# Eleven groups of unread TensorE products taken out ahead of waits, in a two-block float32 model on one core

## The reference, cut to what matters

```
for li in range(2):                                  # first block
    hl = rmsnorm(xl, norm1_g) * (1 + sc1) + sh1
    p  = hl @ w_in                                   # split into latent q, latent kv, rope key, q, k, v, conv
    q  = rmsnorm(p_q, q_norm_g) @ w_uq               # 6 heads of 96
    kv = rmsnorm(p_kv, kv_norm_g) @ w_ukv            # 6 heads, 64 + 64
    a, b, cv = mla(q, kv), swa(...), short_conv(...) # 6 + 6 heads, softmax over up to 512 keys
    xl = xl + g1 * (concat(a, b, cv) @ w_o)
    h  = rmsnorm(xl, norm2_g) * (1 + sc2) + sh2
    aff = softmax(h @ router_w)                      # 16 experts
    top_aff, idx = top_k(aff.T, 32)                  # every expert takes its 32 best tokens
    xl = xl + g2 * scatter(expert_ffn(h[idx]) * top_aff)
x = rmsnorm(xl, final_norm_g)
for layer in range(2):                               # second block
    h = rms_norm(x, norm1_g)
    y = [stick_breaking(h), rwkv7(h), moba(h), hgrn2(h)]
    x = x + (sum over n of sigmoid(h @ w_gate[n]) * (y[n] @ w_branch[n])) @ w_out
    h2 = rms_norm(x, norm2_g)
    x = x + (silu(h2 @ w_ffn_gate) * (h2 @ w_ffn_up)) @ w_ffn_down
return rms_norm(x, final_g)
```

## Time and profile before

| What | Value |
|---|---|
| median of 3 runs | 2405.73 us (2404.16 to 2406.09) |
| the profiled execution's own time | 2400.18 us |
| span of the profiled execution | 2398.1 us |
| TensorE busy | 2207.2 us, 92% of the span |
| VectorE busy | 732.0 us, 31% |
| ScalarE busy | 451.8 us, 19% |
| GpSimd busy | 99.4 us, 4% |
| granted TensorE clock, mean | 0.979 of full |
| moved by DMA | 434.99 MB, mean 181 GB/s |

### The profile page before, as it was taken

One profiled execution on the slowest core, in us unless ns is written; L12 is line 12 of the kernel. 1 busy time (PEld: TensorE's weight loads), 2 busy tenths in 40 slices (PEclk: granted clock), 3 DMA queues, 4 the chain that ended last, 5 costly groups with the idle time before them and its releaser, 6 DMA issues.

```text
span 2398.1 us, 26783 instructions
## 1 busy us (share of the span) xinstructions
PE 2207.2 (92%) x11455; PEld 1605.1 (67%) x11455; DVE 732.0 (31%) x1519; ACT 451.8 (19%) x970; POOL 99.4 (4%) x97
## 2 busy tenths in 40 slices
PE   5898999999889989988798989999999899999998
PEld 2334445665465466544677878888887788888887
DVE  2107723132233731112355423300014444141001
ACT  3003423111121430101134112100003321210000
POOL 1000000000010010000100200000000011000000
PEclk8999999999999999999999999999999999999999
DMA  8532422799922529998532214443543231344352
GB/s 326 208 121 90 151 105 106 311 425 425 415 87 76 176 118 377 427 426 360 186 106 100 100 47 141 141 140 125 157 157 139 72 106 43 120 152 142 124 152 76
DMA packets 172886, 434.99 MB, mean 181 GB/s; under 512 B 6202, under 2 KB 64482, under 8 KB 156130
## 3 DMA queue, kind: packets, MB, share of 16 engines
q1 hardware_dynamic: 171632, 430.90, 48.2%
q10 hardware_dynamic: 1138, 2.39, 0.3%
HBM read 432.23 MB, written 1.05 MB: 181 GB/s over the span
## 4 chain that ended last, share of the span: by engine, by line
PE 78%; DMA 10%; DVE 7%; ACT 3%; issue 1%; POOL 1%; ACTq 0%; DVEq 0%; POOLq 0%
PE bank L274 75%; DMA ring<-in_exp_w_up 4%; DMA ring<-in_exp_w_gate 2%; DMA cst<-in_exp_w_up 1%; PE bank L693 1%; PE bank L518 1%; DMA ring<-in_w_in 1%; POOL arena L578 1%; DVE rstd L602 1%; DMA cst<-in_exp_w_gate 1%; DMA arena<-in_x 1%; DVE arena L658 0%; DVE bank L673 0%; ACT h L597 0%; ACT arena L663 0%
## 5 line engine op out<-in xcount | busy, mean ns | idle before, releaser
L274 PE MATMUL bank<-h,ring 128*128 128x256 f32 (+1 forms) x4064 | 1003.0, 407 | 31.9 <-DMA ring<-in_w_in 11.0
L274 PEld LDWEIGHTS bank<-h,ring 128*128 128x128 f32 x4064 | 770.6, 191 | 249.7 <-issue 128.5
L274 PE MATMUL bank<-arena 128*64 128x256 f32 (+13 forms) x1840 | 325.7, 377 | 51.1 <-ACT arena L663 12.9
L274 PEld LDWEIGHTS bank<-arena 128*128 128x128 f32 (+4 forms) x1840 | 223.2, 193 | 139.3 <-issue 75.8
L274 PE MATMUL bank<-arena,ring 128*128 128x256 f32 x1216 | 264.1, 379 | 6.7 <-DVE arena L2161 3.9
L274 PEld LDWEIGHTS bank<-arena,ring 128*128 128x128 f32 x1216 | 230.3, 190 | 40.5 <-DVE arena L2161 4.7
L663 ACT ACTIVATE arena<-bank 128x256 f32<-128x256 f32 (+5 forms) x265 | 117.6, 461 | 631.1 <-PE bank L274 599.6
L274 PE MATMUL bank<-ring,arena 128*64 128x256 f32 x1344 | 154.3, 384 | 22.1 <-DMA ring<-in_exp_w_up 13.8
L658 DVE COPY arena<-bank 128x256 f32<-128x256 f32 (+7 forms) x116 | 62.3, 539 | 320.3 <-PE bank L274 267.0
L274 PEld LDWEIGHTS bank<-ring,arena 128*64 128x64 f32 x1344 | 97.5, 138 | 85.0 <-DMA ring<-in_exp_w_up 20.3
L578 POOL TENSOR_TENSOR arena<-arena 128x256 f32<-128x256 f32 (+1 forms) x60 | 53.7, 895 | 1805.2 <-ACT arena L571 1803.7
(11 more groups left out here) (278 smaller groups left out, 1466.9 us busy)
## 6 DMA issues: line engine op xcount, KB each, us to landing
ring<-in_w_in SPq DMA_DIRECT2D x32, 2048.0 KB, 7.9
ring<-in_ada_w SPq DMA_DIRECT2D x24, 2048.0 KB, 10.8
ring<-in_exp_w_up SPq DMA_DIRECT2D x22, 2048.0 KB, 15.8
ring<-in_exp_w_gate SPq DMA_DIRECT2D x20, 2048.0 KB, 15.2
ring<-in_exp_w_down SPq DMA_DIRECT2D x20, 2048.0 KB, 16.0
ring<-in_w_ffn_down SPq DMA_DIRECT2D x16, 1408.0 KB, 7.0
ring<-in_w_ffn_gate SPq DMA_DIRECT2D x10, 2048.0 KB, 7.7
ring<-in_w_ffn_up SPq DMA_DIRECT2D x10, 2048.0 KB, 7.7
```

The source lines that it names most:

```text
L274: return PE.matmul(o, lhsT, rhs, start=(k == 0), stop=(k == n - 1))
```

## The change

It deletes `keep_busy` and its eleven calls. Nothing is put in their place.

```
@@ -297,13 +297,6 @@
-        def keep_busy(pe, n):
-
-            b = take(pe, "idle", turn[0])
-            for _ in range(2 * n):
-                mm(b[:, 0:2 * P], ones, cst[:, 0:2 * P], 0, 1)
-            holder[(turn[0] - 1) % rotating[0]] = None
@@ -866,7 +859,6 @@
                 last.then_inc(*tensor.mark("mean", l, name))
-            keep_busy(pe, 4)
             pe.wait_ge(*vector.at("latent", l, "q"))
@@ -911,7 +902,6 @@
             mean_tensor(pe, TQ, ("n2", l))
-            keep_busy(pe, 5 if l < L - 1 else 3)
             join(tensor, pe, ("mixed", l))
@@ -1239,7 +1229,6 @@
                 htok_tensor(pe, l, i)
-            keep_busy(pe, 5)
             pe.wait_ge(*vector.at("pos", l))
@@ -2233,7 +2221,6 @@
                 mean_tensor(pe, S, after_ffn(l))
-                keep_busy(pe, 3)
```

More of the change, by code:

```diff
@@ L299, in take @@
             return banks[b]
[L301 to L306, removed]
         def bank(*key):
```

## The result

| | before | after |
|---|---|---|
| median | 2405.91 us (2404.16 to 2410.88, 4 runs) | 2423.59 us (2421.02 to 2427.55, 4 runs) |
| ratio | | 1.0069, interval 1.0050 to 1.0087 |
| profiled execution, its span | 2400.18, 2398.1 us | 2427.55, 2425.7 us |
| granted clock, mean | 0.979 | 0.961 |

What follows compares the result with a forecast made beforehand. TensorE, with 78% of the chain of waits, was taken to bound the kernel; removed products counted nothing, but half-clock resumes summed to 9.1 us, added to the 2405.73 median for 2414.8 us, range 2409 to 2419.5.

Steps and rivals of the forecast that it cites:

- B: Wait ahead of attention's first scores, layer 0 (225.43 us): newly half clock, late scores delay the attention chain; 1.7 us.
- C: Wait ahead of the router, layer 0 (391.10 us): resume price 1.9 less 0.86 us of ScalarE slack; 1.0 us.
- D: Wait ahead of the dense gather, layer 0 (408.20 us): 1.9 plus 0.1 for small transposes, not absorbed by DMA; 2.0 us.
- F: Wait ahead of the dense latent q products, layer 1 (765.61 us): resume newly at half clock; 1.9 us.
- H: Wait ahead of the router, layer 1 (886.09 us): newly half clock, less 0.33 us of slack; 1.6 us.
- E: Wait after the scatter, layer 0 (681.63 us): ScalarE delivers tiles so slowly that half clock keeps up; 0.
- G: Wait ahead of attention, layer 1 (786.89 us): already resumes at half clock, can only start it earlier; 0.3 us.
- A: Wait ahead of the latent q, layer 0 (197.54 us): already resumes at half clock, so has paid; 0.3 us.
- I: Wait ahead of the gather, layer 1 (899.10 us): already resumes at half clock, so has paid; 0.3 us.
- J: Wait after the scatter, layer 1 (1154.29 us): already 8.73 us idle and half clock before; 0.
- The clock holds through about 5 us: Rival, chance 0.12: only idle times above 6 us cost the clock, C and F, 2.9 us; 2408.6 us.
- Half clock lasts: Rival, chance 0.12: half clock persists through sparse attention and transposes, up to 3 us more in two or three places.

Runs made afterwards that it cites:

- more_all: Against the kernel before: longer unread groups at eight of the eleven waits, plus groups at seven more places; 2387.80 us, ratio 0.9923.
- turns_only: Against the kernel before: the eleven calls still take a bank and a turn but issue no product; 2419.95 us, ratio 1.0067.
- products_only: Against the kernel before: all 90 products stay but take no turn, so later tiles have the changed kernel's banks; 2407.23 us, ratio 1.0001.
- out_d: Against the kernel before: only the unread group at D taken out; 2407.84 us, ratio 1.0006.
- out_aegijk: Against the kernel before: the groups at A, E, G, I, J and at the very end taken out; 2413.25 us, ratio 1.0033.
- out_bcdfh: Against the kernel before: the groups at B, C, D, F and H taken out; 2416.66 us, ratio 1.0043.
- out_b: Against the kernel before: only the group at B taken out; 2408.75 us, ratio 1.0008.
- out_aj: Against the kernel before: only the groups at A and J taken out; 2409.30 us, ratio 1.0010.
- half: Against the kernel before: every unread group has half its products; 2418.24 us, ratio 1.0052.
- more_tails: Against more_all: groups added ahead of the first tokens' wait and the last three heads in the first block's three attentions; 2386.85 us, ratio 0.9921.

## Why the prediction was right or wrong

**Bound and cover: right.** The 90 products cost nothing where they stood. All idle times grew by the group's length with the same releaser, and more_all adds 204 records to the 11455 of before and is 17.5 us faster.

**The banks: right at 0.** turns_only has the whole loss and products_only none of it.

**The clock as the cause: right.** Behind the waits at B, C, D, F and H it is 0.50, or a mean with it, as said. The spans of the eleven traces of the table above reach from 2398.1 to 2425.7 us; less the cost of half clock, 37.8 to 66.9 us, all lie between 2355.1 and 2360.3.

**C, 1.0 forecast, wrong in size.** From 7.82 to 9.37 us for the router and 1.56 up to D. The slack of 0.86 us was taken off a price that was too low, see F.

**D, 2.0 forecast, right:** 1.96 us up to F, E's nothing included. The first 34 records of the gather take 9.85 us in out_d and 10.55 in after instead of 8.50, so 1.35 to 2.05. **E, 0: right**: D to F is 357.05 us in out_aegijk, without E's group, and 357.24 to 357.90 where both stand.

**F, 1.9 forecast, under:** 18.83 for 16.30 us, 2.5. **H, 1.6 forecast, under:** 6.12 for 3.95, 2.2. At both, and at C, the price of one resume was too low. I took it from G, where a mean clock of 0.76 over 7.1 us makes some 3.4 us at half clock, and from the projection at 145.76, 2.11. The 2.5 us at F make some 5.1 us at half clock. These lengths are estimates from the rows.

**B, 1.7 forecast, near in size, by another path:** its own row is 3.2 us longer, but attention, a chain of short waits, takes most of this up; 0.6 us is left. The rest of the 3.35 in the table is more half clock behind it, above all at the end of the context attention, and three of the six traces with B's group in place have that too. On the average B is worth 2.1.

**A, G and I, 0.3 each, and J, 0: the step that failed.** I wrote that A, G and I "already resume at half clock in it and have paid". For A that held: 22.90 against 23.17, and the kernels that keep its eight products show 22.83 to 22.90. For I nearly: 13.08 against 13.86 us, 0.5 to 0.8. For G it was chance. Of the six traces in which G keeps its full group (before, products_only, out_bcdfh, out_b, out_d, out_aj) four have 5.39 us and two 7.08, so as a rule the change takes the clock there too, and with F's it brings on the later fall ahead of the output projection: F to H costs 7.0 us, where 1.9 for F and 0.3 for G stood in the sum. The rows had the warning in them: B kept the clock behind 1.54 us and G lost it behind 1.53, in one trace. J was given nothing because the clock had fallen there already. Its row is 5.30 to 6.75 us without its group and 5.07 to 6.74 with it, so the 1.6 us of after aren't safely J's; and from J to the end out_b and out_bcdfh, with J's group, take the same 1247.3 us as after.

All traces together give the place of the missing microseconds. "With" are the traces that keep the section's groups, "without" those that leave them out (their number in brackets; half is left aside), and the cost is the difference of the two means.

| from, to | groups | with | without | cost, us | forecast |
|---|---|---|---|---|---|
| A, B | A | 27.79 to 27.90 (6) | 27.79 to 28.24 (4) | 0.2 | 0.3 |
| B, C | B | 165.63 to 168.47 (6) | 169.02 to 169.10 (4) | 2.1 | 1.7 |
| C, D | C | 17.10 to 19.11 (7) | 18.66 to 18.70 (3) | 1.3 | 1.0 |
| D, F | D | 357.05 to 357.90 (6) | 358.33 to 359.52 (4) | 1.7 | 2.0 |
| F, H | F, G | 119.21 to 120.53 (5) | 126.74, 126.78 (2) | 7.0 | 2.2 |
| H, I | H | 13.01 to 13.02 (7) | 15.18 to 15.36 (3) | 2.2 | 1.6 |
| I, J | I | 253.67 to 256.01 (6) | 256.08 to 256.91 (4) | 1.2 | 0.3 |
| J, end | J, K | 1243.72 to 1247.34 (6) | 1245.01 to 1247.34 (4) | 1.2 | 0 |
| sum | | | | 16.9 | 9.1 |

16.9 is near the 17.7 between the medians, and 4.8 of the 7.8 us that the forecast lacks lie between F and H. C, H and I, and J perhaps, share the rest; in the last row the two ranges overlap, so its 1.2 us are not shown (one of its four traces, out_aj, keeps K's group).

**The base.** I took the profiled execution of before as the kernel and added the sum to the median. That execution was 5.5 us under the median, which I noted and did not use. It was one in which the clock had held longer at the end of the context attention and where A started early, and the one profiled of after started it late, 6.84 us that the change has no part in. Such luck is in the spans, 27.6 us, and not in the medians, 17.7, against which the forecast's sum is to be held. The scatter of the executions goes with their mean granted clock: of the 76 of before made beside the experiments, the three at 0.973 took 2410.54 to 2413.43 us, the four at 0.980 and over 2397.89 to 2403.59, and the 37 at 0.976 and 0.977 2401.85 to 2411.22. The profiled one had 0.979.

**The range.** It was to end at 2419.5 because "eight such places don't all fall on one side". Six of the eight sections came out over their terms, for one price per resume, and one trace, stood behind them all. That the "some 18" of the dear end lies near the 17.7 is luck: the recorded terms at 3.0 us give about 15.

**The rivals.** *The clock holds through about 5 us:* wrong; it fell at every one of B, D, G and H. *Half clock lasts*, 2421.8 us: nearest in time, and half right in mechanism. The clock came back inside the stretches behind B and G (means of 0.63 and 0.66); it fell again near the end of attention, in layer 1 behind 1.78 us. *The unread work was in the way:* wrong; more unread work made the kernel faster. The Trainium skill's "TensorE: Matmul & The Clock Gate", section "Why this matters for your kernels", asks for idle gaps of at most some 3 us. By the traces C keeps full clock behind 3.22 us (but not in out_aegijk, where its row takes 9.82), H behind 3.67, and D loses it behind 2.35 and 1.16 with a little work between. Neither side of that bound is safe here.

## What to carry to other kernels

Read the granted clock in the stretch behind every wait of TensorE, and read it in several executions: one trace tells which waits can cost the clock, not which do. In these traces an idle time of 1.5 to 3.7 us ahead of dense work cost the clock at some times and not at others, and one of 4.5 us and more did at every place read here. Such a wait is worth filling almost to its end with unread products; half a filling can be worth nothing. And compare the profiled execution with the median before working from its rows: a gap of 5 us between them is itself a finding.

## What the runs showed of the hardware that had not been expected

- Executions of one kernel on one chip scatter by 16 us (2397.89 to 2414.25), 0.7%. The start of A scatters by 9.2 us over eleven kernels with the same program ahead of it, and by 1.9 once the cost of half clock is taken off. more_all, with the waits filled, had 2385.43 to 2388.72, though in 5 runs only.
- Idle time alone doesn't tell whether the clock falls: 3.67 us kept it at H in half, 2.35 + 1.16 us lost it at D, and 1.54 us ahead of G lost it in two traces of six.
- The same wait of 3.04 to 3.27 us for weights left the clock up in five of eleven traces (20.87 us for 48 records) and took it in six (22.25 to 23.87).
- Behind the same idle times the half clock can lie on sparse or on dense work; ahead of and on the output projection that makes a net difference of 1.4 us.
- Half clock behind eleven waits and the bare ones cost 66.9 us of 2425.7 in after, 2.8%. more_tails still has 16.1; what fills the last of it wasn't tried.
